# Sliding-window attention placed between the steps of two dense products, in a two-layer decoder trunk

## The reference

```python
# layer 1
proj = rms_norm(h, mix_norm[1]) @ w_qkv_odd          # 16 query heads, 4 key heads, width 64
q, k, v = split(proj)                                # (L, 16, 64), (L, 4, 64), (L, 4, 64)
# blocks of 128 queries, each against its own and the previous 128 keys
scores = einsum('bntkgd,bnskd->bnkgts', qb, kw) / 8 - slopes * dist    # 0 <= dist < 128, else -inf
m = maximum(max(scores), sink)
pr = exp(scores - m); pr = pr / (sum(pr) + exp(sink - m))
h = h + einsum('bnkgts,bnskd->bntkgd', pr, vw) @ w_o_odd
h = h + square(relu(rms_norm(h, mlp_norm[1]) @ w_mlp_in)) @ w_mlp_out
```

## Time and profile before

| | |
|---|---|
| median of 3 runs | 2778.6 us (2774.49 to 2778.62) |
| the profiled execution | 2777.86 us, of it 2776.1 from the first to the last instruction |
| mean granted TensorE clock | 0.933 |
| TensorE busy | 2527.9 us, 91% |
| DVE, ACT, POOL busy | 1223.5, 534.7, 804.7 us |
| projection, from its first matmul to its last read | 1490.1 to 1625.0 |
| attention, first matmul to the output product | 1637.6 to 1843.6 |
| output product, until the MLP's first matmul | 1843.6 to 1932.1 |

### The profile page before, as it was taken

The page is one execution under the profiler, slowest core; times in us unless marked ns, Lnnn a source line. Parts: engine busy times, 40 slices in busy tenths (PEclk is TensorE's granted clock), DMA queues, the critical chain, the costliest instruction groups (busy, mean ns, idle before and its releaser), DMA issues.

```text
span 2776.1 us, 33670 instructions
## 1 busy us (share of the span) xinstructions
PE 2527.9 (91%) x13070; PEld 2052.9 (74%) x13070; DVE 1223.5 (44%) x1457; ACT 534.7 (19%) x833; POOL 804.7 (29%) x485
## 2 busy tenths in 40 slices
PE   6989874699999999999997966679999999999997
PEld 5878653578888888888876854458888888888885
DVE  5778178933342332424526135533243242333625
ACT  3110033422101001011212025531100101001215
POOL 2312053123233233332222322222332323323320
PEclk9989576799999999999998986789999999999998
DMA  6262231031111111111211232001111111111111
GB/s 190 93 97 88 59 129 63 10 106 46 53 46 48 50 45 53 46 45 53 61 45 46 98 104 56 0 15 46 46 50 48 45 53 45 46 52 46 53 61 61
DMA packets 245370, 166.42 MB, mean 60 GB/s; under 512 B 14520, under 2 KB 230688, under 8 KB 245280
## 3 DMA queue, kind: packets, MB, share of 16 engines
q1 hardware_dynamic: 224160, 132.74, 16.4%
q10 hardware_dynamic: 21136, 32.64, 4.1%
HBM read 136.92 MB, written 27.26 MB: 59 GB/s over the span
## 4 chain that ended last, share of the span: by engine, by line
PE 79%; DVE 12%; ACT 4%; issue 3%; DMA 1%; ACTq 0%; DVEq 0%; SPq 0%; POOLq 0%; POOL 0%
PE ps L516 71%; ACT at_scores L981 1%; PE ps L670 1%; DVE at_scores L1849 1%; DVE softmax_stats L1851 1%; PE ps L668 1%; PE ps L583 1%; DVE s_ba L1385 1%; PE ps L858 1%; DVE s_tmp L1385 1%; DVE s_ca L1385 1%; DVE hg_keys L1621 1%; DVE hg_queries L1622 1%; ACT mid_hi L981 1%; PE ps L949 1%
## 5 line engine op out<-in xcount | busy, mean ns | idle before, releaser
L401 POOL CAST w_hi<-w_raw 128x1024 fp32r<-128x1024 f32 x198 | 211.1, 1066 | 1672.7 <-PE ps L516 1514.2
L516 PE MATMUL ps<-x_hi,w_hi 128*128 128x512 f32 x1760 | 547.3, 392 | 15.7 <-DVE stage L1376 11.5
L516 PE MATMUL ps<-x_lo,w_hi 128*128 128x512 f32 x1760 | 543.9, 390 | 0.0
L516 PE MATMUL ps<-x_hi,w_lo 128*128 128x512 f32 x1760 | 543.2, 390 | 0.0
L403 POOL TENSOR_TENSOR w_lo<-w_raw,w_hi 128x1024 fp32r<-128x1024 f32 x198 | 480.0, 2424 | 15.9
L516 PE MATMUL ps<-mid_hi,w_hi 128*128 128x512 f32 x1312 | 408.3, 393 | 26.6 <-DVE mid_lo L1551 18.9
L516 PE MATMUL ps<-mid_hi,w_lo 128*128 128x512 f32 x1312 | 406.6, 391 | 0.0
L516 PE MATMUL ps<-mid_lo,w_hi 128*128 128x512 f32 x1312 | 406.5, 391 | 0.0
L516 PEld LDWEIGHTS ps<-x_hi,w_hi 128*128 128x128 f32 x1760 | 331.1, 189 | 87.7 <-issue 19.8
L516 PEld LDWEIGHTS ps<-x_lo,w_hi 128*128 128x128 f32 x1760 | 331.6, 188 | 69.6
L516 PEld LDWEIGHTS ps<-x_hi,w_lo 128*128 128x128 f32 x1760 | 331.5, 188 | 69.3
(11 more groups left out here) (243 smaller groups left out, 2186.0 us busy)
## 6 DMA issues: line engine op xcount, KB each, us to landing
w_raw<-w_mlp_in_in SPq DMA_DIRECT2D x64, 512.0 KB, 4.0
w_raw<-w_mlp_out_in SPq DMA_DIRECT2D x64, 512.0 KB, 3.8
w_raw<-w_in_even_in SPq DMA_DIRECT2D x20, 512.0 KB, 4.6
fqig_dram<-stage ACTq DMA_DIRECT2D x16, 512.0 KB, 2.7
w_raw<-w_ple_gate_in SPq DMA_DIRECT2D x16, 512.0 KB, 3.9
w_raw<-w_qkv_odd_in SPq DMA_DIRECT2D x12, 512.0 KB, 3.7
qkv_dram<-stage ACTq DMA_DIRECT2D x12, 512.0 KB, 2.6
x_tokens<-x_in SPq DMA_DIRECT2D x8, 512.0 KB, 7.3
```

The lines of the kernel that those rows point to most:

```text
L401: pool.tensor_copy(WH[:, b, :], RAW[:, b, :]).then_inc(S["w_hi_done"], 1)
L516: ins = pe.matmul(acc[:, h, :], w[:, k, :], x[:, k0 + k, h * HALF:(h + 1) * HALF], start=(k == 0 and w is wh and x is xh), stop=(k == kts ...
```

## The change

The four key heads become two pairs. q, k and v of a pair now lie side by side in the partitions: the columns of the projection are fetched in that order (64 columns at a time for q), so that DVE's read from PSUM puts them where the attention reads them: k and v in the stage tiles ST, q in H. DRAM is not visited. H itself is written to DRAM before, and restored in two halves.

Six units of the projection (the first pair) run as before. Then one list of STEPS_AT = 32 blocks runs without a loop. In steps 0 to 15 TensorE issues, between its attention groups, twice 9 matmuls of the second pair's projection (`other_pair`), which goes by halves of 512 tokens in banks 0 and 1; DVE's `half_read` takes each half. In steps 18 to 33 it issues twice 7 matmuls of `wo_first`: the output product of the first pair's heads, 8 x 2 halves of 12 matmuls; ACT's `part_copy` puts each into PART, and POOL's `add_part` adds it to the restored H. After the last block the other half of the product runs as 8 units of 24 matmuls, and `residual` is as it was. Transposes and outputs run LAG = 2 blocks behind. Scores have one PSUM buffer (banks 4 and 5), the transposes banks 6 and 7.

```diff
--- before.py
+++ after.py
-AT_STEPS = 56
 QH, KVH, HD = 16, 4, 64
-BODY = 2 * NB
-AHEAD = 3
+BLOCKS = 2 * NB
+STEPS_AT = 2 * BLOCKS
+LAG = 2
+V_STEP = 12
...
-UNIT = dict(u=0, heads=4, glu=20, out=24, mlp0=32, gate0=96, up0=104, qkv=112, wo=124, mlp1=132, gate1=196, up1=204)
+UNIT = dict(u=0, heads=4, glu=20, out=24, mlp0=32, gate0=96, up0=104, qkv=112, wo=118, mlp1=126, gate1=190, up1=198)
...
+    SCX = at("at_scores_x", [P, RING, 4, 2 * P], F32, XBH_AT + 16 * K)
+    SCA = at("at_scores_a", [P, RING, 4, 2 * P], F32, XAH_AT)
+    VTX = at("at_v_tokens_x", [P, NB, P], F32, XBL_AT + 16 * K)
+    BIASX = at("at_bias_x", [P, 4, 2 * P], F32, XBL_AT + 24 * K)
...
+    PART = at("wo_part", [P, KT, T], F32, XAL_AT)
...
-            run(SLAB["qkv"], 12, a["w_qkv_odd"][0])
+            def qkv(u):
+                pair, i = divmod(u, 6)
+                b, need = u % 2, SLAB["qkv"] + u - 1
...
+                else:
+                    sp.wait_ge(S["w_ready"], need)
+                    heads = w[:, pair * HALF:(pair + 1) * HALF].rearrange("(k p) (two i c) -> two i p k c", p=P, two=2, i=4)
+                    for two in range(2):
+                        sp.dma_start(RAW[:, b, :].rearrange("p (k n) -> p k n", n=P)[:, :, two * HD:(two + 1) * HD], heads[two, i - 2])\
+                            .then_inc(w_loaded[b], 16)
+            def wo(q):
+                pair, b = q // 4, q % 2
+                sp.wait_ge(S["w_ready"], SLAB["wo"] + q - 1)
+                for two in range(2):
+                    r = pair * HALF + two * 256
+                    sp.dma_start(RAW[two * HD:(two + 1) * HD, b, :].rearrange("p (i n) -> p i n", n=256),
+                                 a["w_o_odd"][0][r:r + 256, q % 4 * 256:(q % 4 + 1) * 256].rearrange("(i c) n -> c i n", c=HD))\
+                        .then_inc(w_loaded[b], 16)
+            def restore(half):
+                sp.wait_ge(S["at_qk_done"], BLOCKS * (half + 1))
+                sp.dma_start(H[:, 4 * half:4 * half + 4, :],
+                             h_dram[half * HALF:(half + 1) * HALF, :].rearrange("(k p) t -> p k t", p=P)).then_inc(S["h_restored"], 16)
+            for u in range(12):
+                qkv(u)
+            wo(0)
+            wo(1)
+            restore(0)
+            for q in range(2, 6):
+                wo(q)
+            restore(1)
+            wo(6)
+            wo(7)
...
+            def add_part(m):
+                pool.wait_ge(S["part_copied"], 2 * m + 2)
+                pool.wait_ge(S["h_restored"], 32 if m < 4 else 48)
+                pool.tensor_tensor(H[:, m, :], H[:, m, :], PART[:, m, :], ALU.add).then_inc(S["h_part"], 1)
+            for g in range(STEPS_AT):
+                normalise(g)
+                if g in (2, 5, 7, 10):
+                    v = (2, 5, 7, 10).index(g)
+                    one(SLAB["qkv"] + 8 + v, 2 * v + 2, "qkv_half_done")
+                if g in (13, 15):
+                    q = (13, 15).index(g)
+                    wo(q, 10 + 2 * q, "qkv_half_done")
+                if g in (21, 24, 28):
+                    q = (21, 24, 28).index(g)
+                    wo(2 + q, 4 * q + 4, "part_done")
+                if g in (23, 24, 26, 28):
+                    add_part((23, 24, 26, 28).index(g))
+            wo(5, 16, "part_done")
+            add_part(4)
+            add_part(5)
+            wo(6, UNIT["wo"] + 2, "acc_done")
+            add_part(6)
+            add_part(7)
+            wo(7, UNIT["wo"] + 4, "acc_done")
...
+            def scores(g):
+                pair, c, n = place(g)
+                lo = P if n == 0 else 0
+                key = ST[2 * pair]
...
+                if g:
+                    pe.wait_ge(S["at_scored"], g)
+                for a_ in range(2):
+                    for two in range(2):
+                        rows = slice(HD * two, HD * (two + 1))
+                        ins = pe.matmul(PS[:, 4 + two, a_ * 256 + lo:(a_ + 1) * 256], H[rows, 4 * pair + 2 * c + a_, n * P:(n + 1) * P],
+                                        key[rows, (n - 1) * P + lo:(n + 1) * P], start=True, stop=True)
+                ins.then_inc(S["at_qk_done"], 1)
...
+            def transposes(g):
+                pe.wait_ge(S["at_norm"], g + 1)
+                if g in (0, V_STEP - LAG):
+                    pe.wait_ge(S["at_vt_copied"], 1 if g == 0 else 2)
+                if g:
+                    pe.wait_ge(S["at_pt_copied"], g)
+                for h in ((1,) if g % NB == 0 else (0, 1)):
+                    for s in range(4):
+                        ins = pe.transpose(PS[:, 6 + h, s * P:(s + 1) * P], scores_at(g)[:, s, h * P:(h + 1) * P], ident[:, :])
+                ins.then_inc(S["at_pt_done"], 1)
+            def outputs(g):
+                n = g % NB
+                pe.wait_ge(S["at_pt_copied"], g + 1)
+                if g >= 2:
+                    pe.wait_ge(S["at_o_done_lo"], g - 1)
+                for two in range(2):
+                    for h in ((1,) if n == 0 else (0, 1)):
+                        ins = pe.matmul(PS[HD * two:HD * (two + 1), 2 + g % 2, 0:256], v_at(g)[:, n - 1 + h, HD * two:HD * (two + 1)],
+                                        probs_at(g)[:, h, 2 * two:2 * two + 2, :], start=(h == 0 or n == 0), stop=(h == 1))
+                ins.then_inc(S["at_o_done"], 1)
...
+            def other_pair():
+                for v in range(6):
+                    s = SLAB["qkv"] + 6 + v
+                    for h in range(2):
+                        if v:
+                            pe.wait_ge(S["qkv_half_read"], 2 * v + h - 1)
+                        if h == 0:
+                            pe.wait_ge(S["w_ready"], s + 1)
+                        for k in range(KT):
+                            for w, x in ((whs[s % 2], XAh), (whs[s % 2], XAl), (wls[s % 2], XAh)):
+                                last = k == KT - 1 and w is wls[s % 2]
+                                ins = pe.matmul(PS[:, h, :], w[:, k, :], x[:, k, h * HALF:(h + 1) * HALF],
+                                                start=(k == 0 and w is whs[s % 2] and x is XAh), stop=last)
+                                if last:
+                                    ins.then_inc(S["qkv_half_done"], 1)
+                                yield
...
+            def v_tokens(pair):
+                if pair:
+                    pe.wait_ge(S["qkv_half_read"], 4)
+                    pe.wait_ge(S["at_pt_copied"], V_STEP - LAG)
...
+            def wo_first():
+                pe.wait_ge(S["at_o_done_lo"], BLOCKS)
+                pe.wait_ge(S["qkv_half_read"], 12)
+                for m in range(KT):
+                    wh, wl = wo_weights(m // 2, m % 2)
+                    if m % 2 == 0:
+                        pe.wait_ge(S["w_ready"], SLAB["wo"] + m // 2 + 1)
+                    for h in range(2):
+                        if m:
+                            pe.wait_ge(S["part_copied"], 2 * m + h - 1)
+                        for k in range(4):
+                            for w, x in ((wh, XBh), (wh, XBl), (wl, XBh)):
+                                last = k == 3 and w is wl
+                                ins = pe.matmul(PS[:, h, :], w[:, k, :], x[:, k, h * HALF:(h + 1) * HALF],
+                                                start=(k == 0 and w is wh and x is XBh), stop=last)
+                                if last:
+                                    ins.then_inc(S["part_done"], 1)
+                                yield
...
+            work = other_pair()
+            for i in range(STEPS_AT + LAG):
+                if i == V_STEP:
+                    v_tokens(1)
+                    dense(work, 9)
+                if i >= LAG:
+                    transposes(i - LAG)
+                if i == BLOCKS + 2:
+                    work = wo_first()
+                if i != V_STEP:
+                    dense(work, 9 if i < BLOCKS else 7)
+                if i + 1 < STEPS_AT:
+                    scores(i + 1)
+                dense(work, 9 if i < BLOCKS else 7)
+                if i >= LAG:
+                    outputs(i - LAG)
+            dense(work, 192)
+            pe.wait_ge(S["at_o_done_lo"], STEPS_AT)
+            pe.wait_ge(S["part_copied"], 16)
+            for m in range(KT):
+                u = UNIT["wo"] + m
+                if m % 2 == 0:
+                    pe.wait_ge(S["w_ready"], SLAB["wo"] + 4 + m // 2 + 1)
+                if m >= 2:
+                    pe.wait_ge(*free_of(u - 2))
+                wh, wl = wo_weights(m // 2, m % 2)
+                unit(ACC[m % 2], wh, wl, XBh, XBl, kts=4, k0=4)
...
+            act.dma_start(h_dram.rearrange("(k p) t -> p k t", p=P), H[:, :, :]).then_inc(S["h_spilled"], 16)
...
+            def part_copy(j):
+                m, h = divmod(j, 2)
+                act.wait_ge(S["part_done"], j + 1)
+                fn(PART[:, m, h * HALF:(h + 1) * HALF], PS[:, h, :], ACT.Copy).then_inc(S["part_copied"], 1)
...
+            v_copy(0)
```

(66 more changed lines are left out.)

279 lines of the change are left out of this document (97 added, 182 removed).

## The result

The changed kernel takes **2682.4 us** (median of 4 runs, 2677.83 to 2683.27) against 2777.7 for the kernel before on the same chip: ratio 0.9656, interval 0.9644 to 0.9668. A second measurement of the same two kernels gave 0.9666 (0.9653 to 0.9679). The forecast was 2677.

A forecast was written before the change was run, and what follows sets the result against it. It took attention as bound by each block's loop latency, no engine full, 6.4 us a block. Terms 3.2 + 112.9 + 13.1 + 82.0 + 13.6 + 46.0 = 270.8 against 372.4, 101.6 us less: forecast 2677, range 2658 to 2722.

The forecast's parts named there:

- The stretch: From the end of the projection's unit 5 to the MLP: 270.8 us against 372.4 in the kernel before.
- start: Before step 0: read of the last unit, eight transposes of v and scores(0), 3.2 us.
- steps 16 and 17, with the cold start behind them: Two steps without dense work: 11.6 us, and 1.5 for a clock that has dropped, 13.1 in all.
- tail: From step 31's start through steps 32 and 33, which have no dense work: 13.6 us.
- second half of the output product: After the attention, 8 x 24 matmuls: 43.5 us, 1.5 for the lower clock, 1 for waits, 46.0.
- The step: One interleaved attention step, TensorE's dense and attention work added: 7.47 us in steps 0 to 15, 6.56 in 18 to 30.
- the switch: TensorE's change between dense and attention matmuls: 0.1 us a step taken, bounds 0 and 0.7.
- The spare time: Slack of the other engines' chain before transposes: 3.6 to 4 us in the first pair, 3 in the second.
- Rival two: Interleaved steps follow the other engines' chain, 1 to 2 us later each: 2706 to 2735 us, chance 0.19.
- Rival four: Interleaving hides nothing; an attention step is the old 6.4 us plus its dense work: 2770 us, chance 0.05.
- Rival three: From attention's start to step 33 TensorE's clock drops; all of it at 1.2 GHz gives 2884 us, chance 0.04.
- The holes: Two gaps of some 5 us on TensorE, in steps 16/17 and after step 31.

The follow-up runs named there:

- spread: The changed kernel with the second pair's projection laid over 18 steps, 16 dense matmuls in each, instead of 18 matmuls over 16 steps: 2678.4 us.
- adds_early: The changed kernel with GpSimd's four late add_parts all issued ahead of the split of wo's column 6: 2676.0 us.
- norm2: The changed kernel with GpSimd making each normalisation twice in a row, so it computes something else: 2697.1 us.
- norm3: The changed kernel with GpSimd making each normalisation three times in a row, so it computes something else: 2729.9 us.
- before_reorder: The kernel before with one edit, ScalarE's out_high issued ahead of the probs copy and the next exponentials, nothing interleaved: 2712.0 us.

## Why the prediction was right

**The stretch.** Predicted 270.8 us, measured 275.4. Term by term:

| | predicted | measured |
|---|---|---|
| start | 3.2 | 3.1 (1559.2 to 1562.3) |
| steps 0 to 15 | 112.9 | 113.8 (to 1676.0) |
| steps 16 and 17, with the cold start behind them | 13.1 | 13.4 (11.9 and 1.5) |
| steps 18 to 30 | 82.0 | 83.0 (to 1772.4, less the 1.5 counted above) |
| tail | 13.6 | 12.0 (to 1784.4) |
| second half of the output product | 46.0 | 50.2 (to 1834.6) |

The 1.5 us of the cold start: from wo_first's first matmul to the next transposes it takes 6.83 us here (1688.50 to 1695.33), and 5.32 in spread, where the clock is full (1688.31 to 1693.63). Up to the second half the sum is right within half a microsecond, 224.8 against 225.2. TensorE is the bound there, so its own work was the right thing to add up; but that it is so close is partly luck, as the steps came out 1.9 us longer than predicted and the tail 1.6 shorter. One error in the steps is the first block of a key head: I took 1.65 us off for it, and in the trace its short groups save 0.42 (scores) and 0.88 (transposes and outputs), 1.3 in all.

**The step**, predicted 7.47 and 6.56, is 7.44 and 6.53, but its parts are not what I took. Eighteen dense matmuls take 2.24 + 2.26 = 4.50 us (1603.28 to 1605.52, 1606.59 to 1608.85), not 4.08, and attention's groups 0.85 + 1.07 + 1.02 = 2.94, not 3.29. The dense matmuls take some 0.4 us a step more, inside my bounds for the switch, and the groups are about as much shorter than the starts in rows 5 had them. Why was not looked into, and starts alone don't tell whether a switch costs 0.4 us or time is only counted to another group. Two errors of 0.4 cancel, and that is luck.

**The spare time** of the other engines: predicted 3.6 to 4 us and 3, the trace has 4.2 (1605.65 to 1609.87) and 3.3, and norm2 and norm3 bracket it. Rival two fell. But my chain already had `out_high` at the head of ScalarE's list ("the end of the step, and its ACT copy: 8.5") without my saying that this is an edit. With the old order it is 36 us slower, 2718.8: rival two would have come true through an edit that my account of the change left out.

**What was wrong** is the reading of the kernel before: "With nothing else to issue, each block of 128 queries pays the latency of the loop". The latency was that of a loop made by the order of two lists, not by the data; before_reorder takes 4.4 us a block on the mean where the kernel before takes 6.4 (full steps 3.54 and 6.20). Rival four rests on that step: it had 2770 for a kernel whose interleaving hides nothing, and the run gives 2721.9. So the forecast was right in size, and the interleaving, which it took for the whole change, accounts for less than half of the gain (39.5 of 95 us) once the list is in its new order. The number didn't suffer from the wrong reading, as it was built from the changed kernel's own work, with the new list in it.

**The term that was mis-sized** is the second half of the output product: "add_part and splits add up to 6 us of waits; I take 1". They cost 4.1: 1.7 and 0.2 us before two units, 2.25 before the MLP; adds_early, in which these waits are gone, lands at 45.3, 0.7 from my 46.0. Behind it the MLP's first unit falls to the lower clock after its first matmuls and takes 12.6 us for 10.9, which my sum didn't hold (the 1.8 us in the last line of the first table). The stretch's 4.6 and this 1.8, less 0.5 by which unit 5 ended sooner, make 2682.2 of the 2676.3 that I had for a profiled execution; it took 2682.13.

**The clock** was 1.00 and 0.98 in the interleaved stretches, the 0.98 with the cold start in it. Rival three, and with it the rule of the Trainium skill, page "TensorE: Matmul & The Clock Gate", section "A second HAM failure mode: psum-queue depth-cycling", did not come about: the kernel changes banks even oftener than the six times a step that I had (nine, by its code, as the scores alternate between banks 4 and 5), but TensorE is busy 114.64 of 115 us, and the small idle times that the rule speaks of are hardly there.

**The holes** were two, as said, with 5.3 and 3.3 us of idle time on TensorE, where I had some 5 each. The first is 12.5 us long, from step 16's first matmul to wo_first's (predicted: 12.1). Inside it a VectorE instruction on four columns takes 2.00 us beside GpSimd's subtract:

```profile
1683.09 2.00 DVE L2008 TENSOR_TENSOR softmax_stats<-softmax_stats 128x4 f32<-128x4 f32 x1
```

```profile
1682.71 2.36 POOL L436 TENSOR_TENSOR w_lo<-w_raw,w_hi 128x1024 fp32r<-128x1024 f32 x1
```

## What to carry to other kernels

Before pricing an overlap, ask of each engine's list what its waiting instruction keeps behind it: a wait of 2.6 us on VectorE in each block, "released by ACT", was a loop between two in-order lists, and moving one copy forward in one list gave 65 us by itself, where the whole change gives 95. Interleaving is best costed by the bound engine's own work per step, with the spare time of the other engines checked against it; but to know what it brings, compare it with the same kernel without it, not with the kernel before. At the seams, lay small work of GpSimd where VectorE is idle, and dense work into every step.

## What the runs showed of the hardware

- A VectorE operation with two inputs in SBUF takes 3.41 us instead of 1.22 while GpSimd runs its adds or the subtract of a split (3.42), and the one on four columns 2.00 us instead of 0.15: it ends at 1685.09, GpSimd's subtract at 1685.07. In the changed kernel's attention seven operations on four columns (lines 2002, 2003 and 2008) take from 0.35 to 2.31 us where 0.15 or 0.16 is the rule; each ends 0.01 to 0.03 us after a split's or an add's instruction on GpSimd, as 1766.11 to 1768.42 beside an add that ends at 1768.40. GpSimd is held up too: two adds took 6.73 us, 3.4 each, where four that lay beside almost nothing of VectorE's took 9.40, 2.35 each. The Trainium skill, page "VectorE: DVE Perf Modes", section "Two Vector instructions with no wait between them", speaks of a read interface that VectorE shares with GpSimd; the trace agrees. What was new to me is that a tiny instruction waits as well, for the rest of GpSimd's.
- An idle time of 2.25 us was followed by a lower clock soon after: the MLP's matmuls start at 0.70 and 0.62 us for a pair, then take 0.97 and three times 1.06, then 0.62 again. After an idle time of 0.59 (adds_early, 1842.84) or 2.29 (spread, 1688.31) they did not slow down in the matmuls read here. Why 2.25 us cost the clock and 2.29 didn't, these runs don't settle.

```profile
1834.65 0.70 PE L579 MATMUL ps<-x_hi,w_hi 128*128 128x512 f32 x2 [2.25 <-issue]
...
1836.42 1.06 PE L579 MATMUL ps<-x_hi,w_hi 128*128 128x512 f32 x2
...
1839.99 0.62 PE L579 MATMUL ps<-x_hi,w_lo 128*128 128x512 f32 x2
```
